# A two-block transformer kernel: the router's two searches as one row of groups and experts, and the projection of p moved from the routing into expert pairs 9 to 12

## What is computed

```python
def hierarchical_moe(h, w_group, b_group, w_router, b_router, w_gate, w_up, w_down):
    g_logits = t @ w_group + b_group                      # 4 groups
    g_w, g_idx = lax.top_k(softmax(g_logits), 1)
    e_logits = einsum('td,gde->tge', t, w_router) + b_router   # 4 x 8 experts
    e_sel = take_along_axis(e_logits, g_idx)              # the chosen group's 8
    e_val, e_idx = lax.top_k(e_sel, 2)
    e_w = softmax(e_val) * g_w
    ...                                                   # the 2 experts' outputs, weighted
x = x + hierarchical_moe(rmsnorm(x, g_ffn), ...)
gate = sigmoid(rmsnorm(x, g_ple) @ w_ple_gate)
x = x + gate * (p @ w_ple_proj)                           # p: 256 x 256, w_ple_proj: 256 x 1024
```

## Time and profile before

| what | value |
|---|---|
| median of three runs | 951.76 us (950.13 to 953.07) |
| span of the profiled execution | 949.0 us |
| PE busy | 921.4 us, 97% |
| DVE, ACT, POOL busy | 501.4, 330.9, 36.0 us |
| PE's share of the chain that ended last | 86% |
| DMA | 289.45 MB, mean 305 GB/s |
| granted clock of TensorE, mean | 0.995 |

### The profile page before, as it was taken

One profiled execution on the slowest core, in us unless ns is written; L12 is line 12 of the kernel. 1 busy time (PEld: TensorE's weight loads), 2 busy tenths in 40 slices (PEclk: granted clock), 3 DMA queues, 4 the chain that ended last, 5 costly groups with the idle time before them and its releaser, 6 DMA issues.

```text
span 949.0 us, 14172 instructions
## 1 busy us (share of the span) xinstructions
PE 921.4 (97%) x5886; PEld 650.6 (69%) x5886; DVE 501.4 (53%) x867; ACT 330.9 (35%) x528; POOL 36.0 (4%) x39
## 2 busy tenths in 40 slices
PE   7999999999999899999999999999999999999997
PEld 6997734443444445334344389989999999999886
DVE  7784612221222312222222199999898977766642
ACT  6832210101011000001101088556566755644541
POOL 1000000000000000000000000123220000000000
PEclk9999999999999999999999999999999999999999
DMA  9997799999999999999999984643433435554301
GB/s 334 407 388 311 302 387 430 424 431 430 430 430 432 428 427 431 429 430 430 430 430 422 422 357 177 246 163 126 168 134 144 178 111 194 227 202 178 134 1 44
DMA packets 28981, 289.45 MB, mean 305 GB/s; under 512 B 3056, under 2 KB 6384, under 8 KB 12400
## 3 DMA queue, kind: packets, MB, share of 16 engines
q1 hardware_dynamic: 28192, 286.91, 74.0%
q10 hardware_dynamic: 720, 1.57, 0.4%
HBM read 287.43 MB, written 1.05 MB: 304 GB/s over the span
## 4 chain that ended last, share of the span: by engine, by line
PE 86%; DVE 8%; ACT 3%; issue 2%; DMA 0%; DVEq 0%; POOL 0%; ACTq 0%
PE ps L279 85%; DVE wl L275 3%; PE ps L1081 1%; ACT wh L268 1%; DMA arena<-in_xT 0%; ACT arena L1903 0%; DVE arena L393 0%; DVE arena L1944 0%; DVE arena L2015 0%; DVE ple_l L1477 0%; ACT h_h L1449 0%; DVE arena L1486 0%; DVE mg_l L1951 0%; ACT arena L1906 0%; DVE mix_l L624 0%
## 5 line engine op out<-in xcount | busy, mean ns | idle before, releaser
L279 PE MATMUL ps<-ring,arena 128*64 128x512 f32 x1216 | 340.2, 600 | 5.9 <-issue 5.9
L275 DVE TENSOR_TENSOR wl<-ring,wh 128x1024 fp32r<-128x1024 f32 x150 | 181.5, 1243 | 40.2 <-ACT wh L268 40.1
L279 PEld LDWEIGHTS ps<-ring,arena 128*64 128x64 f32 x1216 | 109.1, 138 | 125.0 <-issue 123.2
L268 ACT ACTIVATE wh<-ring 128x1024 fp32r<-128x1024 f32 x150 | 151.9, 1053 | 43.2 <-PE ps L279 30.4
L279 PE MATMUL ps<-arena 128*64 128x512 f32 (+4 forms) x448 | 158.4, 522 | 0.5 <-DVE arena L1173 0.3
L1186 DVE SCALAR_TENSOR_TENSOR arena<-ps,arena 128x512 f32<-128x512 f32 x16 | 12.0, 752 | 205.0 <-PE ps L279 205.0
L279 PEld LDWEIGHTS ps<-arena 128*64 128x64 f32 (+2 forms) x448 | 54.7, 144 | 86.6 <-issue 82.1
L279 PE MATMUL ps<-up_h,wh 128*128 128x256 f32 x352 | 85.7, 282 | 0.7 <-ACT up_h L2004 0.7
L279 PE MATMUL ps<-up_l,wh 128*128 128x256 f32 x352 | 82.3, 280 | 0.0
L1256 ACT ACTIVATE y_h<-ps 128x512 fp32r<-128x512 f32 x32 | 19.0, 597 | 151.7 <-PE ps L279 151.7
L279 PEld LDWEIGHTS ps<-up_h,wh 128*128 128x128 f32 x352 | 66.3, 188 | 0.9 <-issue 0.9
(11 more groups left out here) (279 smaller groups left out, 1466.3 us busy)
## 6 DMA issues: line engine op xcount, KB each, us to landing
ring<-in_moe SPq DMA_DIRECT2D x69, 2048.0 KB, 23.6
arena<-in_moe SPq DMA_DIRECT2D x17, 2048.0 KB, 23.6
ring<-in_w_in SPq DMA_DIRECT2D x12, 2048.0 KB, 9.7
ring<-in_w_up SPq DMA_DIRECT2D x11, 2048.0 KB, 7.6
ring<-in_moe SPq DMA_DIRECT2D x24, 512.0 KB, 15.3
ring<-in_w_dn SPq DMA_DIRECT2D x5, 2048.0 KB, 8.1
ring<-in_w_out SPq DMA_DIRECT2D x4, 2048.0 KB, 16.1
arena<-in_moe SPq DMA_DIRECT2D x8, 512.0 KB, 13.9
```

The lines of the kernel that those rows point to most:

```text
L268: e.activation(wh(i), raw_piece(i), ACT.Copy).then_inc(*hi.up(i))
L275: e.tensor_tensor(wl(i), raw_piece(i), wh(i), SUB).then_inc(*lo.up(i))
L279: return e.matmul(o, l, r, start=first, stop=final, skip_group_check=True)
```

## The change

The router's logits become 40 columns: four for the groups, four that are filled (weights 0, bias -1e30), and 32 for the experts. Over two tiles that is ten rows of eight. One `first_max` finds in all ten the maximum and its one-hot OH1: the group, and the best expert of every group. The winners are then covered with -1e30 (E2, 64 wide) and a second `first_max` finds each group's second best (OH2). The sum of OH1 and OH2 is multiplied by the group's one-hot `goh` to give the mask. The difference of the two values is formed for all groups, multiplied by goh and summed to `dv`, behind the mask and ahead of `x1_lo`. The flag's two operations move into `count_dve`, behind the first pick. On ACT, `x1_hi` of the second half comes ahead of the exponentials.

`project_p` leaves `route_pe` and stands behind the first part of the scatter of pairs 9, 10, 11 and 12, a quarter in each, into bank 4; ACT copies each behind the pair's two copies of the output, and `down_turn` of the next pair waits for that copy. The load of w_pp moves behind (g, 8) and waits for the first block's output projection, since it lands where PP lies; the weights are ordered by quarters.

```diff
-        wr = ctx.enter_context(nc.sbuf_tensor("wr", [128, 8, 36], F32))
+        wr = ctx.enter_context(nc.sbuf_tensor("wr", [128, 8, 40], F32))
...
-        PPW = A(o + 2560, 2, 1024)
+        PPW = A(4096, 4, 2, 256)
...
+        PQ = (9, 10, 11, 12)
+        def project_p(e, h):
+            if h == 0:
+                e.wait_ge(l_xk, 32)
+                e.wait_ge(l_pT, 16)
+            for y in range(2):
+                for c in range(2):
+                    k = mm(e, ps[4][:, y * 256:y * 256 + 256], PPW[:, h, c, y * 128:y * 128 + 128], PT[:, c, :], c == 0,
+                           c == 1)
+            k.then_inc(*ppm.up(h))
...
         def route_pe(e):
-            e.wait_ge(l_xk, 32)
-            e.wait_ge(l_pT, 16)
-            for h in range(3):
-                project_p(h)
             e.wait_ge(*masked.at(0))
...
-            project_p(3)
...
         def route_act(e):
+            x1_hi(e, 1)
             e.wait_ge(*gmax.at("neg"))
...
-            x1_hi(e, 1)
-            for h in range(4):
-                if h == 3:
-                    e.wait_ge(*gap.at(0))
-                    e.activation(ex, dv, ACT.Exp).then_inc(*egap.up(0))
-                e.wait_ge(*ppm.at(h))
-                e.activation(PP[:, 2 * h:2 * h + 2, :].rearrange("p a b -> p (a b)"), ps[PB[h]][:, :],
-                             ACT.Copy).then_inc(*pp.up(h))
+            e.wait_ge(*gap.at(0))
+            e.activation(ex, dv, ACT.Exp).then_inc(*egap.up(0))
...
-            first_max(GL, 4, gm, goh, gmin)
+            first_max(LGX, 10, mx1, OH1X, mn1)
             e.tensor_scalar(ngm, gm, -1.0, None, M).then_inc(*gmax.up("neg"))
             e.wait_ge(*vc.at())
-            for i in range(2):
-                e.tensor_tensor(em[:, i], EL[:, i], goh[:, i, :].unsqueeze(2).to_broadcast([128, 4, 8]),
-                                M).then_inc(*vc.up())
+            e.scalar_tensor_tensor(out=E2, in0=OH1[:, :, 8:40], scalar=-1e30, in1=LG[:, :, 8:40], op0=M,
+                                   op1=ADD).then_inc(*vc.up())
+            e.wait_ge(*vc.at())
+            first_max(E2X, 8, v2.rearrange("p i g -> p (i g)"), OH2X, mn2)
+            e.wait_ge(*vc.at())
+            e.tensor_tensor(E2, OH1[:, :, 8:40], OH2, ADD).then_inc(*vc.up())
...
-                e.tensor_reduce(es[:, i, :], em[:, i].rearrange("p g e -> p e g"), AX, ADD).then_inc(*vc.up())
+                k = e.tensor_tensor(mask[:, i], comb[:, i], goh[:, i, :].unsqueeze(2).to_broadcast([128, 4, 8]), M)
+            k.then_inc(*masked.up(0))
+            e.tensor_tensor(gap4, v2, v1, SUB).then_inc(*vc.up())
             e.wait_ge(*vc.at())
-            first_max(es, 8, v1, oh1, e1min)
+            e.tensor_tensor(gap4, gap4, goh, M).then_inc(*vc.up())
             e.wait_ge(*vc.at())
-            e.scalar_tensor_tensor(out=e2, in0=oh1, scalar=-1e30, in1=es, op0=M, op1=ADD).then_inc(*vc.up())
-            e.wait_ge(*vc.at())
-            first_max(e2, 8, v2, oh2, e2min)
-            e.tensor_tensor(dv, v2, v1, SUB).then_inc(*gap.up(0))
...
+            e.tensor_reduce(dv, gap4, AX, ADD).then_inc(*gap.up(0))
             x1_lo(e, 1)
...
             e.tensor_scalar(pos, pos, -1.0, None, ADD).then_inc(*slots.up(0))
+
+        def count_dve(e):
             e.tensor_reduce(cm, ps[3][:, 64:96], AX, ALU.max).then_inc(*vc.up())
...
-                    if q == 0:
-                        e.wait_ge(*pp.at(3))
...
+                if q - 1 in PQ:
+                    e.wait_ge(*pp.at(PQ.index(q - 1)))
...
                 scatter(q, 0)
+                if q in PQ:
+                    project_p(e, PQ.index(q))
...
             pick(0)
+            count_dve(e)
...
+                if q in PQ:
+                    h = PQ.index(q)
+                    e.wait_ge(*ppm.at(h))
+                    e.activation(PP[:, 2 * h:2 * h + 2, :].rearrange("p a b -> p (a b)"), ps[4][:, :],
+                                 ACT.Copy).then_inc(*pp.up(h))
...
-                if (name, n) == ("d", 0):
-                    e.dma_start(PPW, dr["w_pp"][0].rearrange("p (c n) -> p c n", c=2)).then_inc(l_xk, 16)
+                if (name, n) == ("g", 8):
+                    e.wait_ge(*proj.at("out1", 1, 1))
+                    e.dma_start(PPW.rearrange("p h c n -> p (h c n)"), dr["w_pp"]).then_inc(l_xk, 16)
```

More of the change, by code:

```diff
@@ L421, in build @@
         MIXH, MIXL = rounded("mix_h", 6144, 8, 256), rounded("mix_l", 4096, 8, 256)
-        LB = SM[:, 0:36]
+        LB = SM[:, 0:40]
         RT, VS, VM, VV, R2 = (SM[:, x:x + 2] for x in (40, 42, 44, 46, 48))
@@ L780, in two @@
             return small(2 * n).rearrange("p (i n) -> p i n", i=2)
-        LG = two(36)
-        GL, EL = LG[:, :, 0:4], LG[:, :, 4:36].rearrange("p i (g e) -> p i g e", g=4)
-        gm, goh, gmin = small(2), two(4), small(2)
-        ngm, gex, gs = small(2), two(4), small(2)
[L786 to L790, removed]
+        lg_, oh1_ = small(80), small(80)
+        LG, LGX = lg_.rearrange("p (i n) -> p i n", i=2), lg_.rearrange("p (x e) -> p x e", e=8)
+        OH1, OH1X = oh1_.rearrange("p (i n) -> p i n", i=2), oh1_.rearrange("p (x e) -> p x e", e=8)
+        goh = OH1[:, :, 0:4]
+        mx1 = small(10)
+        gm, v1 = mx1.rearrange("p (i g) -> p i g", i=2)[:, :, 0], mx1.rearrange("p (i g) -> p i g", i=2)[:, :, 1:5]
+        mn1, v2, mn2 = small(10), two(4), small(8)
+        ngm, gex, gs = small(2), two(4), small(2)
+        e2, oh2_ = small(64), small(64)
+        E2, E2X = e2.rearrange("p (i n) -> p i n", i=2), e2.rearrange("p (x e) -> p x e", e=8)
+        OH2, OH2X = oh2_.rearrange("p (i n) -> p i n", i=2), oh2_.rearrange("p (x e) -> p x e", e=8)
+        gap4 = two(4)
         dv, ex = small(2), small(2)
-        inb = two(8)
         mask = small(64).rearrange("p (i g e) -> p i g e", i=2, g=4)
@@ L796, in build @@
         cm = small(1)
-        comb = small(64).rearrange("p (i g e) -> p i g e", i=2, g=4)
+        comb = e2.rearrange("p (i g e) -> p i g e", i=2, g=4)
         cb = comb.rearrange("p i g e -> p i (g e)")
-        den, w1, w2, inn = small(2), small(2), small(2), two(8)
+        den, w1, w2 = small(2), small(2), small(2)
         RW = small(4).rearrange("p (k n) -> p k n", k=2)
@@ L870, in route_dve @@
             for i in range(2):
-                e.scalar_tensor_tensor(out=LG[:, i, :], in0=ps[3 + i][:, 0:36], scalar=R2[:, i:i + 1], in1=LB, op0=M,
+                e.scalar_tensor_tensor(out=LG[:, i, :], in0=ps[3 + i][:, 0:40], scalar=R2[:, i:i + 1], in1=LB, op0=M,
                                        op1=ADD).then_inc(*logit.up(i))
@@ L2400, in _layout @@
     pp = i["w_ple_proj"][0]
-    r["w_pp"] = _cols(pp, 1)
+    r["w_pp"] = np.ascontiguousarray(pp.reshape(2, 128, 4, 256).transpose(1, 2, 0, 3)).reshape(128, -1)
     r["w_pg"] = np.ascontiguousarray(i["w_ple_gate"][0].reshape(8, 128, 2, 4, 128).transpose(2, 1, 3, 0, 4)).reshape(2, 128, -1)
```

43 lines of the change are left out of this document (14 added, 29 removed).

## The result

The changed kernel takes 959.52 us (median of four runs, 958.65 to 960.72), the kernel before 951.39 (four runs, 950.13 to 953.07). The ratio is 1.0093, 95% interval 1.0080 to 1.0105: **slower by 0.9%**, where 955.5 was predicted and 958.0 was the end of the range. The profiled spans are 958.4 and 949.0 us, so +9.4 where the sum said +3.7.

A forecast was written before the change was run, and what follows sets the result against it. PE's own work, racing a full weight stream, was taken as the bound; -0.84 (gather's start) + 1.7 (half clock in the gather) + 2.86 (pairs) = +3.7 us, giving a median of 955.5 us, range 952.3 to 958.0.

The forecast's parts named there:

- The search: Routing on DVE, up to the mask: the new chain takes 3.49 us, 0.99 less than the 4.48 before.
- Rival 4: Routing search on DVE: width eats what fewer steps save, the chain stays at 4.48 us; sum +4.7, 956.5 us; chance 3%.
- Behind the mask: From mask to gather: DVE late, 0.3 us lost, 0.16 won by moving the flag; gather's start -0.84 us with the search.
- Rival 1: Routing: the clock holds, gather at 1.00, 1.7 us off the sum; +2.0, 953.8 us; chance 20%.
- The gather: Gather after the routing: begins at 1.2 GHz since PE idled, +1.7 us; bounds 0 and 3.8.
- The branch at pair 8: Overflow-flag branch at pair 8: PE's hole of 3.67 us noted in the profile, no term in the sum.
- The pairs: Pairs 9 to 13: four quarters add 7.03 us, pair 13's wait of 2.25 and half clock of 1.92 go; +2.86 us.
- rival 3: End of the pairs: the weight stream sets the end, not PE; sum +2.5, 954.3 us; chance 10%.
- The end: From the last down half to the kernel's end: no term in the sum, forecast 0.

The follow-up runs named there:

- after_busy: The changed kernel with useless matmuls keeping PE at work in the routing, and 4 transposes in a never-run branch body: 951.11 us, ratio 1.0011.
- before_pad: The kernel before with 46 more transposes in PE's never-run branch body of pair 8: 950.95 us, ratio 1.0004.
- before_pad95: The kernel before with 95 more transposes in PE's never-run branch body of pair 8: 953.43 us, ratio 1.0028.
- quarter_alone: The kernel before, old search, with only the projection's fourth quarter moved behind pair 12, its weights loaded ahead of the full stream: 951.89 us, ratio 1.0020.
- after_pad: The changed kernel with 16 more transposes in PE's never-run branch body of pair 8: 953.8 us, ratio 1.0042.
- best: The kernel before with the new search and only the projection's fourth quarter moved, behind pair 12, the others staying in the routing: 948.82 us, ratio 0.9980.
- busy_pairs_empty: after_busy with each projection quarter in pairs 9 to 12 cut to one two-column matmul, the projection left out: 951.52 us, ratio 1.0013.
- busy_front: after_busy without the useless matmuls behind the count, and with eight more never-run transposes: 953.65 us, ratio 1.0027.

## Why the prediction was wrong, point by point

**The search: right.** 3.48 us for 3.49, from the rows of widths 8, 16 and 256. Rival 4, by which the width eats what the steps save, is out: a step took 0.23 to 0.24 us at 80 elements and 0.22 to 0.23 at 64, for 0.17 at 16. The prediction called that rival the page's case, and read only half of the section for it: the Trainium skill, "VectorE: DVE Perf Modes", in the section on the TRN2 errata, says right below its table that the row with 58 cycles is too low for single operations, and gives (N + 151)/0.96 ns for an fp32 tensor_tensor of N elements. By that an estimated 0.24, 0.22 and 0.17 us at 80, 64 and 16, which the traces bear out.

**Behind the mask: wrong in who is late.** I had DVE late by 0.3 us, and forecast the count at half clock nowhere, though I said in the next part that PE would have idled 4 us by then, and took half clock for the gather. It cost 1.05 us in the count. So the gather started 0.10 us earlier and not 0.84. Rival 1 (the clock holds) is out.

**The gather: right in kind, short in size.** 2.50 for 1.70: it stayed at half clock for all but its last four matmuls. I had taken the prices of two holes from the earlier trace rows, in stretches of large matmuls, where the clock came back sooner. The bound of 3.8 us was too far: with a matmul every 0.21 us for 0.12, a gather wholly at half clock costs an estimated 2.9 us.

**The branch at pair 8: the failed step.** It was not a term of the sum. I named the first hole, said that the code branches there, and took its 3.67 us as the same before and after. It was +5.0 us: 2.98 and 4.42 us of standing, and half clock behind them. The hole itself was a row that asked for a cause: PE stood for nothing that the profile shows, behind a taken branch, with its instructions in another block. The change takes 64 instructions of PE from ahead of it, and every change of PE's program ahead of a branch moves the target within its block. A rival for it, with the two holes, would have given about 960.

**The pairs: right.** +2.71 for +2.86: four quarters of 1.7 us, the wait and the half clock at pair 13 gone, no new wait. From pair 9's gate half to the end it is 592.4 us in the changed kernel and 592.3 in after_busy, so the delay ahead did not make these pairs dearer. What it changes is what taking the quarters out would bring: nothing in after_busy, where the stream sets the end without them (the case of rival 3), and by the spare more in the changed kernel.

**The end: not forecast, -0.91.** PE's wait of 1.00 us behind the last block in the earlier trace rows is 0.61 us now, but the stage behind it begins as long after the last down half as before (11.11 us for 11.13), so that gave nothing. From profile to profile this stretch varies by more than 0.91: it is 408.9 us in the kernel before and 410.9 in before_pad, which differ in instructions that never run. Its cause stays open.

**Range and chances.** The range ended at the sum of the bounds of the terms that I had. The terms that I had listed came to +5.1 as measured, which is inside; what was outside was the term not listed.

## What to carry to other kernels

A matmul that hides behind another engine is not free to remove: where its removal leaves PE idle ahead of dense work (0.57 and 1.00 us did no harm here, 1.55 and 1.58 did), ask what half clock costs there, and move only as much as the other engine's chain has become shorter. Behind every branch that is taken, look for the hole that the profile gives no cause for, count how many instructions stand between the target and its block's edge, and expect it to change with any edit ahead of it; instructions in a body that never runs moved it at no cost here. And a delay on PE is worth what the next wait for a load leaves of it: 5.3 us at pair 9 were 3.1 at the end in one kernel, 7 us of matmuls were nothing in another.

## What the runs showed of the hardware

- PE stood for 3.0 to 3.7 us behind a taken branch in all fourteen kernels, with the DMA queues full. PE went on 2.6 to 2.7 us after the packet of the instruction queue started, in all of them. A second wait came where little was left in the target's block: 4.42 and 3.31 us with 2 matmul records left, 1.89 with 7, 0.43 with 15.
- The length of a hole alone did not decide on the clock. Behind the branch 3.61 and 3.67 us brought the half clock (before_pad, before), and 3.27 in after_busy, and even 3.18 (before_pad95), but 3.11, 3.20 and 3.25 (quarter_alone, after_pad, best) did not; ahead of pair 13's up half 2.25 and 2.58 did, but 2.59 in busy_pairs_empty, 1.66 and 1.83 did not; in the routing 1.55 and 1.58 did, 0.57 did not. The Trainium skill, "TensorE: Matmul & The Clock Gate", Part 1, says that the number of slow matmuls at a start varies between runs of one kernel; the two groups of times of busy_front agree with such a thing for the fall as well.
- Once down in the routing, the clock stayed at 0.50 for 10.2 us in the changed kernel and after_pad, across ten records of 32 columns, an idle stretch and most of a dense gather; in busy_front, with dense work alone behind its hole, it was at 0.50 from 107.4 to 110.8 us only.
